# A two-layer hybrid decoder trunk on one core: negated maximum in one step, sine products on GpSimd, the last block's top-k by its dropped keys, new order tables, and pre-added residual tiles for the layer norms

## The chip, the core and the metric

The kernel runs on one core of a Trainium2 chip. The metric is the device time of one execution in microseconds (us), as a median over several runs. The profile is one execution, recorded by the hardware profiler. Engines are named as in the profile: PE is TensorE (PEld its weight loads), DVE is VectorE, ACT is ScalarE, POOL is GpSimd, SP is SyncE. A letter q behind a name (DVEq, POOLq) is that engine's instruction queue.

## The reference

There are 1024 tokens of width 1024 and two layers. A layer mixes the tokens in three groups of heads that read one input projection, maps the result by an output projection, and applies a layer norm. An MLP of width 4096 with squared ReLU and a gated input embedding follow, and a second layer norm. What the change touches is this, cut from the reference:

```
def layer_norm(x, g, b):
    mu = xf.mean(-1, keepdims=True)
    var = jnp.square(xf - mu).mean(-1, keepdims=True)
    return ((xf - mu) * lax.rsqrt(var + LN_EPS) * g + b)

def rotary(x, cos, sin):
    x1, x2 = jnp.split(x, 2, axis=-1)
    return concatenate([x1 * cos - x2 * sin, x2 * cos + x1 * sin])

def block(args):                       # 128 queries
    logits = einsum('bqhd,bsd->bqhs', iqb, ik) * IDX_DIM ** -0.5
    score = einsum('bqhs,bqh->bqs', relu(logits), iwb)
    score = where(causal, score, -inf)
    _, sel = lax.top_k(score, 256)     # 256 keys for each query
    s = einsum('bqhd,bqkd->bqhk', qb, k_sel) * HEAD_DIM ** -0.5
    pr = softmax(where(valid, s, -inf))
    return einsum('bqhk,bqkd->bqhd', pr, v_sel)

x = layer_norm(ALPHA * x + mix, ln1_g, ln1_b)
x = layer_norm(ALPHA * x + ffn + ple, ln2_g, ln2_b)
```

The other two groups of heads are a delta-rule state update over time (RWKV-7) and a pooling mixer. The change leaves their code alone, except for when their input columns are computed.

## The kernel before, in words

Activations lie transposed: features on the 128 partitions, the 1024 tokens along the free dimension in two halves of 512. Each layer is a row of stages with a meeting of all engines between them.

**The mix stage.** The input projection `z` has 17 tiles of 128 features, each done for two halves, and each half in four parts of two matmuls (`z_part`). The attention goes by blocks of 128 queries; block b sees (b+1)*128 keys. Blocks 0 and 1 see at most 256 keys and need no search. The others are searched in the order 3, 4, 5, 6, 7, 2 (`TOP_ORDER`), so block 2, with 384 keys, comes last. What is done for a block has short names:

- `iq` and `q`: PE computes the indexer's queries or the attention's queries; ACT copies them to QZ, and four DMAs on ACT's queue write them to QZS with the halves of each head swapped; DVE (`rotate`, L1589 to L1601) multiplies QZ by the cosines (L1598), QZS by the sines (L1599) and adds the two (L1601). DVE waits for the swapped copy before the first of the three.
- `lg`: for each of 8 indexer heads PE computes logits (L651), ACT takes ReLU and weight (L1212, L1220), POOL adds them up in SC (`scores`, L1379).
- `round`: DVE finds the 8 greatest of the scores (MAX8, L1611) and overwrites them with -1e30 in WK (L1613, two records: a load of the 8 values and the replacement). 32 rounds find 256 keys (`topk_round`).
- `bias`: POOL (L1469, L1471), or DVE for block 2 (L1745, L1747), turns WK and SC into 0 for a chosen key and -1e30 for another.
- `s`, for each of 6 heads: PE computes attention scores (L664). DVE (`maximum`, L1627 to L1632) adds the bias, writes the sum to PB and takes its maximum to MX, then multiplies that one column by -1/8 to NM (L1631). ACT takes the exponential with NM as bias (L1103). `pt`: PE transposes the probabilities (L671), ACT copies them (L1109). `pv`: PE multiplies by the values (L678).
- `inv`, `fin`, `sq`, `ss`, `norm`: the division by the softmax sums (L1637, L1644, L1646), the sum of squares over heads (PE L698), and the RMS norm on DVE (L1655, L1660), which reads square roots that ACT takes in two steps.
- `shift`: POOL's token shift and pooling on z tiles from the fourth on.

The order of all of it on each engine is written out in four tables (`TENSOR_ORDER`, `SCALAR_ORDER`, `VECTOR_ORDER`, `POOL_ORDER`). An engine goes through its table in that order and waits at each item for its semaphores. The buffers QZ and QZS exist once for `iq` and once for `q`; attention scores and logits share two wide PSUM buffers, one for even and one for odd heads.

**The other stages.** Preparation, the state update in 8 steps, the output projection, a layer norm, the gate, an MLP in 8 groups of 512 hidden features, and a second layer norm. The projections there split each fp32 operand into a high and a low part and use three matmuls (L1021 to L1023). DVE reads each result bank and adds it to the residual Y: L1852 behind the output projection, L1884 in the MLP; each such instruction covers one of 8 tiles for one half. POOL makes the low part of each weight block (L1502).

**The layer norm**, five times in a run (one before the first layer): PE takes the mean by 8 accumulating matmuls of the mean matrix with Y for each half (L601). DVE subtracts it (L1525). ACT squares the first half's tiles, POOL the second half's (L1353); PE adds the squares (L606), ACT takes the square root (L1072), DVE the reciprocal (L1532), and a chain of multiplications on DVE and ACT gives the result. PE does both halves' means before the first sum of squares:

```
for hf in range(2):
    for kt in range(KT):
        mm = e.matmul(BK_[4 + hf], mean_ones, Y[:, kt, hs(hf)], start=kt == 0, stop=kt == KT - 1)
    mm.then_inc(ln_mu, 1)
for hf in range(2):
    for kt in range(KT):
        e.wait_ge((ln_sq, ln_sq_later)[hf], u * KT + (kt + 1))
        e.matmul(BK_[6 + hf], mean_ones, SQ[:, 2 * hf + kt % 2, :], ...)
```

## Time and profile before

| | us |
|---|---|
| median of 3 runs | 3779.99 |
| lowest and highest | 3774.95, 3780.49 |
| the profiled execution, its own time | 3774.45 |
| its span, first to last instruction | 3772.6 |
| PE busy | 3427.3 (91% of the span) |
| DVE busy | 1784.7 (47%) |
| POOL busy | 1121.2 (30%) |
| ACT busy | 1068.7 (28%) |
| mean granted clock of TensorE | 0.954 of full |

In us from the start of the span, the mix stage of the first layer lies at 63 to 621, its state update at 660 to 872, its output projection at 903 to 1002, its two layer norms behind 1002 and behind 1866; the mix stage of the second layer lies at 1913 to 2474. The share of busy time is an average over stages that have different limits, so the rows below are mostly of one stage each. Matmul records overlap one another, and fp32 matmuls leave two records each.

### The profile page before, as it was taken

How to read it: one execution, taken by the hardware profiler on the slowest of the kernel's cores; microseconds unless marked ns; L12 is line 12 of the kernel's file. 1: busy time of each engine (PE TensorE's matmuls, PEld its weight loads, DVE VectorE, ACT ScalarE, POOL GpSimd, SP SyncE). 2: the span in 40 equal slices, each digit the busy share in tenths (PEclk: the TensorE clock that was granted, in tenths of full speed). 3: DMA queues.
4: the chain of work that ended last, by engine and by line, in shares of the span. 5: the costliest groups of instructions: out<-in, count | busy, mean ns of one | idle time of the engine just before them, and what ended most of it. 6: DMA issues, size and time to landing. Idle time of an engine off the chain costs nothing.

```text
span 3772.6 us, 61018 instructions
## 1 busy us (share of the span) xinstructions
PE 3427.3 (91%) x23080; PEld 2462.0 (65%) x23080; DVE 1784.7 (47%) x3061; ACT 1068.7 (28%) x1875; POOL 1121.2 (30%) x940
## 2 busy tenths in 40 slices
PE   7889887898999999999988888779889999999997
PEld 3444444886667888888734445458765688888884
DVE  5689996344342222222348899844335122222224
ACT  3343224443122111122133432244412112122122
POOL 1274341651212222222114543335412222222221
PEclk9999998998999999999999998889999999999998
DMA  3100000000101111111111000000011111111111
GB/s 119 38 27 22 19 20 18 1 0 20 59 12 56 50 50 44 44 53 47 34 49 39 11 22 21 18 19 0 1 34 49 35 51 44 50 45 50 50 39 45
DMA packets 43864, 132.74 MB, mean 35 GB/s; under 512 B 9280, under 2 KB 11840, under 8 KB 43072
## 3 DMA queue, kind: packets, MB, share of 16 engines
q1 hardware_dynamic: 37280, 122.41, 10.0%
q10 hardware_dynamic: 6432, 8.40, 0.9%
q8 instruction: 84, 1.38, 0.2%
q14 instruction: 68, 0.56, 0.1%
HBM read 117.15 MB, written 5.24 MB: 32 GB/s over the span
## 4 chain that ended last, share of the span: by engine, by line
PE 59%; DVE 14%; DVEq 11%; issue 10%; ACT 2%; POOLq 2%; POOL 1%; ACTq 1%; DMA 0%; SPq 0%
PE bank L1021 14%; PE bank L1023 14%; PE bank L1022 14%; DVEq L1615 8%; DVE M L1611 8%; PE bank L751 3%; PE bank L629 2%; PE wide L601 2%; DVE PB L1627 2%; PE wide L751 1%; PE wide L606 1%; DVEq L1612 1%; DVE WK L1613 1%; PE bank L719 1%; POOLq L1503 1%
## 5 line engine op out<-in xcount | busy, mean ns | idle before, releaser
L1502 POOL TENSOR_TENSOR WL<-WR,WH 128x1024 fp32r<-128x1024 f32 x160 | 389.8, 2436 | 1492.0 <-ACT WH L1305 1491.3
L629 PE MATMUL bank<-X,WR 128*128 128x512 f32 x1088 | 532.2, 633 | 19.2 <-ACT A L1189 9.9
L1021 PE MATMUL bank<-XH,WH 128*128 128x512 f32 x1280 | 517.4, 404 | 19.8 <-DVE XL L1548 10.2
L1023 PE MATMUL bank<-XH,WL 128*128 128x512 f32 x1280 | 501.5, 392 | 0.0
L1022 PE MATMUL bank<-XL,WH 128*128 128x512 f32 x1280 | 501.5, 392 | 0.0
L1884 DVE TENSOR_TENSOR Y<-Y,bank 128x512 f32<-128x512 f32 x256 | 175.9, 687 | 492.1 <-PE bank L1023 492.1
L1021 PE MATMUL bank<-HH,WH 128*128 128x512 f32 x1024 | 400.4, 391 | 0.0
L1023 PE MATMUL bank<-HH,WL 128*128 128x512 f32 x1024 | 398.6, 389 | 0.0
L1022 PE MATMUL bank<-HL,WH 128*128 128x512 f32 x1024 | 398.4, 389 | 0.0
L629 PEld LDWEIGHTS bank<-X,WR 128*128 128x128 f32 x1088 | 206.0, 200 | 270.6 <-issue 243.8
L1305 ACT ACTIVATE WH<-WR 128x1024 fp32r<-128x1024 f32 x160 | 168.2, 1053 | 736.3 <-PE bank L1023 727.7
L1871 DVE TENSOR_TENSOR RB<-RB 128x512 f32<-128x512 f32 x128 | 88.5, 692 | 561.1 <-ACT RB L1331 561.1
L1611 DVE MAX8 M<-WK 128x8 f32<-128x512 f32 (+5 forms) x372 | 331.6, 891 | 23.0 <-issue 0.9
L1613 DVE MATCH_REPLACE8 WK<-M,WK 128x512 f32<-128x512 f32 (+5 forms) x372 | 325.8, 876 | 2.3 <-issue 2.3
L1021 PEld LDWEIGHTS bank<-XH,WH 128*128 128x128 f32 x1280 | 242.2, 189 | 85.9 <-DVE XL L1548 19.7
L1022 PEld LDWEIGHTS bank<-XL,WH 128*128 128x128 f32 x1280 | 242.4, 189 | 56.5 <-issue 7.7
L1023 PEld LDWEIGHTS bank<-XH,WL 128*128 128x128 f32 x1280 | 242.2, 189 | 51.4
L1379 POOL TENSOR_TENSOR SC<-SC,R 128x512 f32<-128x512 f32 (+5 forms) x84 | 141.2, 1681 | 295.2 <-ACT R L1220 279.5
L1021 PEld LDWEIGHTS bank<-HH,WH 128*128 128x128 f32 x1024 | 192.2, 188 | 45.7 <-DVE HL L1875 6.4
L1331 ACT ACTIVATE RB<-bank 128x512 f32<-128x512 f32 x128 | 76.5, 598 | 511.2 <-PE bank L1023 511.2
L1023 PEld LDWEIGHTS bank<-HH,WL 128*128 128x128 f32 x1024 | 192.2, 188 | 40.4
L1022 PEld LDWEIGHTS bank<-HL,WH 128*128 128x128 f32 x1024 | 192.2, 188 | 39.6
(275 smaller groups left out, 5141.7 us busy)
## 6 DMA issues: line engine op xcount, KB each, us to landing
WR<-in_w SPq DMA_DIRECT2D x128, 512.0 KB, 3.5
WR<-in_w_in SPq DMA_DIRECT2D x34, 512.0 KB, 3.5
WR<-in_w_out SPq DMA_DIRECT2D x16, 512.0 KB, 3.5
WR<-in_w_gate SPq DMA_DIRECT2D x16, 512.0 KB, 5.8
Y<-in_xT SPq DMA_DIRECT2D x2, 2048.0 KB, 13.1
out_T<-X SPq DMA_DIRECT2D x1, 4096.0 KB, 11.8
QZS<-QZ ACTq DMA_DIRECT2D x48, 64.0 KB, 2.0
QZS<-QZ ACTq DMA_DIRECT2D x64, 48.0 KB, 2.0
```

The source lines that it names most:

```text
L629: mm = e.matmul(BK_[hf], WR[:, i % RING, kt, :], X[:, kt, hs(hf)], start=kt == 0, stop=kt == KT - 1)
L751: mm = e.matmul(BK_[bank][chunk(c), j * CH:(j + 1) * CH], lhs[chunk(c), 2 * j + g, :], rhs[chunk(c), 2 * j + g, :], start=True, stop=True)
L1021: e.matmul(BK_[b], WH[:, s, w, :], high[:, kt, q], start=kt == 0, stop=False)
L1022: e.matmul(BK_[b], WH[:, s, w, :], low[:, kt, q], start=False, stop=False)
L1023: mm = e.matmul(BK_[b], WL[:, s, w, :], high[:, kt, q], start=False, stop=kt == kts - 1)
L1305: e.activation(WH[:, split_seq(i) % 2, :, :], WR[:, i % RING, :, :], ACT.Copy).then_inc(w_high, 1)
L1379: e.tensor_tensor(SC[:, sl, 0:n], SC[:, sl, 0:n], R[:, w, 0:n], ALU.add).then_inc(relu_used, 1)
L1502: e.tensor_tensor(WL[:, s, :, :], WR[:, i % RING, :, :], WH[:, s, :, :].bitcast(F32), ALU.subtract)
L1611: e.max(M8[:, :], src)
L1613: e.match_replace(work, M8[:, :], src, BIG)
L1615: e.drain()
L1884: e.tensor_tensor(Y[:, i, hs(hf)], Y[:, i, hs(hf)], BK_[b], ALU.add).then_inc(d_free[b], 1)
```

## The change

Four things change in the mix stage, and one around the layer norms.

1. **Negated maximum in one step.** The instruction at L1627 scales by -1/8 and takes the minimum, so that it writes the negated maximum to NM itself. The column multiplication at L1631 goes; the drain before it stays and now signals `max_ready`.
2. **Sine products on GpSimd.** `rotate` is split: `iqc`/`qc` is the cosine product (DVE no longer waits there for the swapped copy), `iq`/`q` in DVE's table is the sum. The sine product is an item of POOL's table.
3. **Dropped keys in the 384-key block.** For block 2, the scores are copied negated and reversed to WK, and 16 rounds find the 128 keys that are dropped; one instruction turns this into the bias, reading WK reversed.
4. **New order tables** for all four engines.
5. **Residual tiles pre-added.** Behind each result read by DVE in the output projection and in the MLP, DVE also adds the Y tile to a running sum for its half (7 additions for each half; in all 8 groups of the MLP, the last of which counts). PE then takes each half's mean by one matmul of that sum, in four of the five layer norms.

```
-            def layer_norm(u, landed=None):
+            def layer_norm(u, landed=None, sums=None, total=None):
...
+                    else:
+                        e.wait_ge(ln_sum, sums + (hf + 1))
+                        mm = e.matmul(BK_[4 + hf], mean_ones, total[:, hf, :], start=True, stop=True)
...
-                for b in range(4):
-                    e.wait_ge(d_free[b], L * D_USES + (N_WOUT // 2 + 1))
-                layer_norm(L * 2 + 1)
+                layer_norm(L * 2 + 1, sums=L * LN_SUMS, total=RB)
...
-                for b in range(4):
-                    e.wait_ge(d_free[b], L * D_USES + (D_USES + 1))
-                layer_norm(L * 2 + 2)
+                layer_norm(L * 2 + 2, sums=L * LN_SUMS + 2 * FB, total=RST)
...
+            def add_to_sum(total, kt, hf):
+                if kt == 0:
+                    return
+                e.drain()
+                q = hs(hf)
+                ins = e.tensor_tensor(total[:, hf, :], Y[:, 0, q] if kt == 1 else total[:, hf, :], Y[:, kt, q], ALU.add)
+                if kt == KT - 1:
+                    ins.then_inc(ln_sum, 1)
...
POOL
+                    elif kind in ("iq", "q"):
+                        e.wait_ge(tables_landed, L * 32 + 32)
+                        e.wait_ge(swapped[kind], 64 * (rotations(L, (kind, b)) + 1))
+                        e.tensor_tensor(QZS[:, k, 0:n, :], QZS[:, k, 0:n, :], spread(ST[:, b * P:(b + 1) * P], n),
+                                        ALU.mult).then_inc(sined[kind], 1)
...
rotate, on DVE
-                e.wait_ge(swapped[kind], 64 * (rotations(L, use) + 1))
-                e.tensor_tensor(dst[:, :, :], QZ[:, k, 0:n, :], spread(CT[:, q], n), ALU.mult)
-                e.tensor_tensor(QZS[:, k, 0:n, :], QZS[:, k, 0:n, :], spread(ST[:, q], n), ALU.mult)
-                e.drain()
+                if part == "cos":
+                    e.wait_ge(turned.free, turned.read(L, use))
+                    e.tensor_tensor(dst[:, :, :], QZ[:, k, 0:n, :], spread(CT[:, q], n), ALU.mult)
+                    e.drain()
+                    return
+                e.wait_ge(sined[kind], rotations(L, use) + 1)
                 e.tensor_tensor(dst[:, :, :], dst[:, :, :], QZS[:, k, 0:n, :], ALU.add).then_inc(rotated[kind], 1)
...
topk_round
+                drop = b == TOP_ORDER[-1]
+                src = work if i or drop else SC[:, s, 0:n]
+                    if drop:
+                        e.tensor_scalar(work, SC[:, s, 0:n][:, ::-1], -1.0, None, ALU.mult)
+                        e.drain()
-                e.match_replace(work, M8[:, :], src, BIG)
-                if i < ROUNDS - 1:
+                e.match_replace(work, M8[:, :], src, DROPPED if drop else BIG)
+                if i < (ROUNDS // 2 if drop else ROUNDS) - 1:
...
maximum
-                e.tensor_tensor_reduce(out=PB[:, w, 0:n], in0=WIDE[w][:, 0:n], in1=bias, scale=1.0,
-                                       scalar=-3e38, op0=ALU.add, op1=ALU.max, accum_out=MX[:, b, h:h + 1])\
+                e.tensor_tensor_reduce(out=PB[:, w, 0:n], in0=WIDE[w][:, 0:n], in1=bias, scale=-HD ** -0.5,
+                                       scalar=3e38, op0=ALU.add, op1=ALU.min, accum_out=NM[:, b, h:h + 1])\
                  .then_inc(wide[w].free, 1)
-                e.drain()
-                e.tensor_scalar(NM[:, b, h:h + 1], MX[:, b, h:h + 1], -HD ** -0.5, None, ALU.mult)\
-                 .then_inc(max_ready, 1)
+                e.drain().then_inc(max_ready, 1)
...
bias of block 2, on DVE
-                        e.tensor_tensor(work, work, SC[:, SLOT[b], 0:n], ALU.subtract)
-                        e.drain()
-                        e.tensor_scalar(work, work, 0.0, BIG, ALU.is_equal, ALU.mult)
+                        e.tensor_scalar(SC[:, SLOT[b], 0:n], WK[:, SLOT[b], 0:n][:, ::-1], DROPPED, BIG, ALU.is_equal,
+                                        ALU.mult)
...
the end of DVE's table, before and after
-    s.7.4 s.7.5 q.2 round.2 inv.7 round.2*6 fin.7 bias.2 s.2.0 s.2.1 norm.3 norm.4 norm.5 s.2.2 s.2.3 norm.0 norm.1
-    s.2.4 norm.7 s.2.5 norm.6 inv.2 fin.2 norm.2
+    round.2*5 s.7.0 s.7.1 round.2*7 s.7.2 s.7.3 round.2*4 bias.2 s.7.4 s.7.5 qc.2 q.2 inv.7 fin.7 s.2.0 s.2.1
+    s.2.2 s.2.3 norm.5 norm.0 norm.1 s.2.4 s.2.5 norm.6 inv.2 norm.7 fin.2 norm.3 norm.4 norm.2
```

## Rows read from the trace of the kernel before

**Rows 1.** The page's chain that ended last, by engine.
```profile
PE 59%; DVE 14%; DVEq 11%; issue 10%; ACT 2%; POOLq 2%; POOL 1%; ACTq 1%; DMA 0%; SPq 0%
```

**Rows 2.** Windows: start:end, length, busy us (instructions) by engine, PE clock, DMA, GB/s.
```profile
63.00:621.00 558.00, 472.22 (x1824) 249.73 (x1824) 453.69 (x833) 189.90 (x329) 222.33 (x173) 0.92 0.09 28
...
490.00:540.00 50.00, 45.52 (x160) 22.71 (x160) 46.30 (x69) 10.30 (x20) 16.84 (x13) 1.00 0.09 25
540.00:588.00 48.00, 33.07 (x192) 23.15 (x192) 42.20 (x105) 14.24 (x20) 15.44 (x14) 0.86 0.04 12
588.00:624.00 36.00, 23.49 (x110) 12.84 (x110) 22.67 (x61) 18.46 (x39) 7.96 (x7) 0.86 0.10 26
```

**Rows 3.** PE's waits, 110 to 588 us: sum, times, longest.
```profile
PE wide L671 <- ACT PB L1103: 50.8, 22, 8.1
```

**Rows 4.** DVE, one mix stage, by form: busy us, mean ns, idle before.
```profile
L1611 DVE MAX8 M<-WK 128x8 f32<-128x384 f32 x31 | 17.3, 558 | 2.0
L1613 DVE MATCH_VALUE_LOAD WK<-M,WK 128x8 f32 x186 | 17.1, 92 | 13.6
L1613 DVE MATCH_REPLACE8 WK<-M,WK 128x384 f32<-128x384 f32 x31 | 16.8, 542 | 0.0
...
L1631 DVE TENSOR_SCALAR NM<-MX 128x1 f32<-128x1 f32 x48 | 7.4, 154 | 4.5
...
L1599 DVE TENSOR_TENSOR QZS<-QZS,ST 128x512 f32<-128x512 f32 x6 | 6.5, 1086 | 0.0
...
L1599 DVE TENSOR_TENSOR QZS<-QZS,ST 128x384 f32<-128x384 f32 x8 | 5.5, 684 | 0.0
...
L1745 DVE TENSOR_TENSOR WK<-WK,SC 128x384 f32<-128x384 f32 x1 | 0.5, 548 | 0.0
...
L1747 DVE TENSOR_SCALAR WK<-WK 128x384 f32<-128x384 f32 x1 | 0.4, 360 | 0.1
```

**Rows 5.** DVE's timeline, two maxima and the next round: start, duration.
```profile
120.20 0.15 DVE L1631 TENSOR_SCALAR NM<-MX 128x1 f32<-128x1 f32 x1
120.39 0.29 DVE L1627 CUSTOM_DVE_ANT_0 PB<-wide,C 128x128 f32<-128x128 f32 x1
120.61 0.08 DVE L1627 DVE_READ_ACCUMULATOR2_ANT MX<- 128x1 f32 x1
120.78 0.15 DVE L1631 TENSOR_SCALAR NM<-MX 128x1 f32<-128x1 f32 x1
120.85 0.68 DVE L1611 MAX8 M<-WK 128x8 f32<-128x512 f32 x1
```

**Rows 6.** The tile QZS: sums of a rotation, ns min/median/max.
```profile
L1601 DVE TENSOR_TENSOR QT<-QT,QZS x16: 557/558/1421, 91.5 to 2430.6; 128x384 f32<-128x384 f32 x16
```

**Rows 7.** DVE's timeline at the end of the mix stage.
```profile
575.07 1.22 DVE L1627 CUSTOM_DVE_ANT_0 PB<-wide,WK 128x1024 f32<-128x1024 f32 x1
...
587.70 0.42 DVE L1644 TENSOR_TENSOR A<-bank,SPR 128x256 f32<-128x256 f32 x1 [0.27 <-issue]
...
589.53 0.56 DVE L1627 CUSTOM_DVE_ANT_0 PB<-wide,WK 128x384 f32<-128x384 f32 x1 [0.30 <-issue]
```

**Rows 8.** Timelines of the layer norm at 1002 us: PE, then DVE.
```profile
1003.23 13.97 PE L601 MATMUL wide<-Y,C 128*128 128x512 f32 x32 [0.87 <-DVE Y L1852]
1017.04 9.32 PE L606 MATMUL wide<-SQ,C 128*128 128x512 f32 x20
...
1002.39 0.69 DVE L1852 SCALAR_TENSOR_TENSOR Y<-X,bank 128x512 f32<-128x512 f32 x1 [4.75 <-PE bank L1023]
...
1010.37 4.87 DVE L1525 TENSOR_TENSOR Y<-Y,wide 128x512 f32<-128x512 f32 x8 [7.29 <-PE wide L601]
...
1025.30 3.35 DVE L1532 RECIPROCAL RST<-STD 128x512 f32<-128x512 f32 x1 [3.20 <-ACT STD L1072]
```

**Rows 9.** All lines of the run: busy us, mean ns, idle before.
```profile
L1502 POOL TENSOR_TENSOR WL<-WR,WH 128x1024 fp32r<-128x1024 f32 x160 | 389.8, 2436 | 1492.0 <-ACT WH L1305 1491.3 <-issue 0.7
...
L1884 DVE TENSOR_TENSOR Y<-Y,bank 128x512 f32<-128x512 f32 x256 | 175.9, 687 | 492.1 <-PE bank L1023 492.1
```

124 lines of the change are left out of this document (64 added, 60 removed).

## The prediction

> **What bounds the kernel now.** I read the chain that ended last first: PE holds 59% of it, DVE and its queue 25% [rows 1]. So two engines set the end, each in stages of its own. The windows show where DVE does. In the mix stage, 558 us long, DVE is busy 453.7 us and PE 472.2; from 540 to 588 us DVE has 42.2 of 48 us and PE 33.1 [rows 2]. What DVE lacks there is mostly spacing between instructions: a round of the search shows 0.07 us between two of them [rows 4]. Once the rounds have begun, near 110 us, DVE is the queue that never empties. PE's own waits in that stretch confirm it: 50.8 us are waits of the transposes for the exponential [rows 3], which waits for DVE's maximum. I take the second layer's stage as equal.
>
> The reader should see a second thing in the windows: PE is not far behind. From 490 to 540 us it has 45.5 of 50 us [rows 2].
>
> In the MLP and in the output projection PE is the bound, and DVE waits for each bank: 492.1 us before 256 additions, 1.9 us each [rows 9]. In the layer norm the bound is a chain through several engines. PE takes 13.97 us for 32 records of the means, and only then comes the first sum of squares, at 1017.04; the first reciprocal starts at 1025.30 [rows 8].
>
> **The change part by part, one mix stage.**
>
> *Rounds.* One round on 384 keys is 0.558 + 0.092 + 0.542 us, with spacings of 2.0/31 and 13.6/186 us [rows 4]: 1.33 us. 16 fewer are 21.3 us off DVE's queue.
>
> *Bias and reversal of block 2.* The subtraction goes (0.548 us with 0.07 spacing), the reversed copy comes. No row has a reversed read. Its bounds are L1747's 0.36 us and L1745's 0.55 us [rows 4]; I take 0.5, and this edit is worth nothing.
>
> *Negated maximum.* L1631 costs 0.154 us and 0.09 idle, 48 times: 11.9 us is the most. But the drain stays. Start to start, L1631 holds up the next maximum by 0.19 us and the next round by only 0.07 us, since a round's first instruction starts before it ends [rows 5]. I count 24 of each kind: 6.2 us. The lower bound is 48 times 0.07, or 3.4 us.
>
> *Sine products.* Six of 512 columns at 1.086 us and eight of 384 at 0.684 us [rows 4], less 0.08 us overlap each: 10.9 us. These means hold collisions. An undisturbed product of 384 columns takes 0.56 us, as the median of the sums shows [rows 6], and then the saving is some 7.5 us (estimate, scaled by columns). The collisions will now hit the cosines and sums, so I take 10. On POOL the 14 products are about 1.3 us each, at the mean of its 173 instructions (222.3 us, rows 2): 18 us on an engine that is 40% busy there. They are hidden behind DVE's rounds if POOL comes to them in time. POOL waits for the four swap DMAs instead of DVE, and its next `lg` or `shift` items queue behind that wait; PE waits for the sum before `lg` and `s`.
>
> A sum of a rotation sometimes takes 1.42 us instead of 0.56 [rows 6], while a round keeps its time beside a busy POOL (mean 558 ns over 31, rows 4). So only some of DVE's instructions are held up by POOL. The Trainium skill (SBUF — State Buffer, the section on the shared port) says the pair of ports of DVE and GpSimd is an exclusive lock, taken when a DVE instruction has two SBUF inputs and GpSimd reads SBUF, and its Perfetto Trace Analysis page warns that moving work between the two might not help. By that rule the 14 new POOL products could block DVE's sums or cosines, but not the rounds; the rows agree on both. What it could cost is a rival below.
>
> *Together* 21.3 + 6.2 + 10 = 37.5 us less on DVE. Not all of it shortens the stage. Before, eight rounds and more lay between block 7's last maximum (575.07 to about 576.4) and its `fin` at 587.70, and hid the chain exponential, transpose, copy, `pv`, `fin`; that last one did not wait for PE [rows 7]. In the new table only a rotation and a reciprocal lie there, so this chain is open. It is at most 11.3 us; I take 7.5. DVE then needs about 8.9 us to reach block 2's first maximum, where its own work is 2.3: 6.6 us exposed. That leaves 30.9. The tail behind 589.53 lasts some 34 us. Block 2's first four maxima now come ahead of the norms, and less of `z` stands between its transposes: I put 4 us (0 to 8). PE must do its 472 us in about 526, 90% instead of 85%: I charge 3 us for maxima that come late. **32 us for each stage**, 64 for two.
>
> **The layer norms.** In front of the norm at 1002 us, DVE reads the last bank at 1002.39 [rows 8]. With the change it adds 0.69 us, a drain of 0.07 and the running sum of another 0.69: 1003.85. The first half's sum has long been done, so its mean (now one matmul in place of eight, about 0.9 us) is ready by then, and centring starts at 1003.9, not 1010.37. The greater gain is behind: the squares' matmuls no longer wait for the second mean. Before, 8.3 us passed from the first of them (1017.04) to the reciprocal (1025.30). Now the first square is there after one subtraction and one square, 1.4 us (estimate), so 1005.3 + 8.3 = 1013.6. DVE is through with its 16 subtractions at 1003.9 + 2 x 4.87 = 1013.6 too. So the reciprocal starts near 1013.8: **11.5 us earlier**. POOL's squares and everything behind shift along. Four such norms: 46 us. The norm in front of the first layer keeps its code.
>
> The additions cost nothing where they stand: 14 for each group, 0.69 us plus drain. The MLP's idle of 1.9 us before each addition [rows 9] covers them, and the output projection's 4.75 us [rows 8] more so. If POOL's weight split of 2.44 us [rows 9] stood in their way, a bank would come free some 2 us later; PE has three other banks meanwhile. Without this cover each would cost 0.76 us. The last one is in the sum above.
>
> **Sum.** 64 + 46 = 110 us. Against the profiled execution's 3774.45 that gives 3664.5. The median stands 5.5 us (0.15%) above that execution; I put **3668 us** for the median, 3% less.
>
> **Rivals.**
>
> *PE becomes the bound of the mix stage (0.20).* For: PE's best stretch is 91% [rows 2], and the new stage asks for 90% on average, with an order in which each transpose waits for an exponential. Against: PE's largest waits are for DVE [rows 3] and should shrink. If PE keeps only 87%, a stage lasts 472/0.87 = 543 us and gives 15 us: 30 + 46 = 76, or about 3700.
>
> *All of DVE's saving arrives (0.10).* The open chain is covered by the new order, and the tail gives 8 us: 45 us a stage, 136 in all, about 3640.
>
> *The layer norm's PE runs at the lower clock (0.10).* The stretch 540 to 588 us, where PE is busy 33 of 48 us, has a granted clock of 0.86 against 1.00 in the fuller one before it [rows 2]. The 13.97 us of dense means go, so the sums of squares could run at 1.2 GHz. They take 0.43 us a record now (9.32 over 20 has 0.4 idle, rows 8); at half the clock the first half's 16 take 13.8 us instead of 6.9. Each norm then gives 4.6 us, 18 in all, with 64: about 3694. The Trainium skill (TensorE: Matmul & The Clock Gate, Part 1) says that the gate halves the clock when the array has recently been idle; by it this rival is possible, and no row shows it for this place.
>
> *The shared ports (0.04).* Each of 28 rotations loses a POOL product's 1.3 us: 36 us back, about 3704.
>
> *Slower: POOL's queue (0.03).* The sine product stands behind `lg`, `bias` and `shift` items in one queue. If DVE has to wait for six POOL instructions of 1.3 us at each of 28 rotations, that is 28 x 7.8 = 218 us against 110: about 3885. It decides from 3.9 us per rotation on. Against: POOL is idle 60% of the stage [rows 2], and a rotation can be asked for early.
>
> *My forecast* has 0.53.
>
> **How the numbers follow.** The unknown terms of the forecast (maximum 3.4 to 11.9, sines 7.5 to 10.9, chain, tail 0 to 8, PE) make it 3648 to 3686. With the rivals at 3640 and 3700 inside, the range is 3634 to 3708. A measurement of this kernel can tell some 0.2% (7.6 us) from no change. Faster by more than that: all cases but the last, less a little for what I have overlooked, 0.96; within it 0.015; slower 0.025.
>
> **What would show it.** In the changed profile: 186 searches reduced to 170 in each stage; no L1631 records; DVE's busy time in a mix stage near 417 us, its length near 526; a wait of DVE of some 6 us before block 7's `fin`; the means as 4 records of PE and a first reciprocal 11.4 us behind the last bank, in place of 22.9; PE's wait for the exponential below 50.8 us. It is wrong if DVE shows waits for POOL's sine products, if PE has over 92% of the stage, or if the first reciprocal of a norm comes later than 14 us behind the last bank.

## The result, and the profile after

The changed kernel takes **3711.36 us** (median of 4 runs, 3705.19 to 3717.18), beside 3779.55 (3774.95 to 3780.49) for the kernel before in the same comparison: ratio 0.9823, 95% interval 0.9811 to 0.9835. That is 68 us faster. The forecast was 3668 in a range of 3634 to 3708, so the sign was right, the size was not, and the median lies outside the range. The profiled execution has a span of 3710.5 us at a mean granted clock of 0.951. One slow execution, of n_middve (5609 us at a mean granted clock of 0.553), is left out of that kernel's median below.

The layer norms' part of the forecast, 46 of 110 us, came in almost to the tenth. The timelines of VectorE and of TensorE at a changed layer norm (start, duration, engine, line, operation), which answer to [rows 8]:

```profile
996.02 0.69 DVE L1872 SCALAR_TENSOR_TENSOR Y<-X,bank 128x512 f32<-128x512 f32 x1 [3.97 <-PE bank L1028]
996.80 0.69 DVE L1566 TENSOR_TENSOR RB<-RB,Y 128x512 f32<-128x512 f32 x1
997.41 9.65 DVE L1532 TENSOR_TENSOR Y<-Y,wide 128x512 f32<-128x512 f32 x16
1007.18 3.35 DVE L1539 RECIPROCAL RST<-STD 128x512 f32<-128x512 f32 x1
...
995.82 1.02 PE L606 MATMUL wide<-RB,C 128*128 128x512 f32 x2
997.55 1.12 PE L606 MATMUL wide<-RB,C 128*128 128x512 f32 x2 [0.71 <-DVE RB L1566]
998.81 9.42 PE L611 MATMUL wide<-SQ,C 128*128 128x512 f32 x20
```

The means are 4 records instead of 32. The first reciprocal starts 1007.18 - 996.02 = 11.2 us behind the last bank, where it started 1025.30 - 1002.39 = 22.9 behind it: 11.75 us gained, 11.5 forecast. The other three changed norms are alike (11.2 or 11.3 us behind the last bank, 22.9 or 23.0 before), and the granted clock during the sums of squares is 1.00 in both kernels.

The mix stage is the other half. Its last row before the next stage is the setting of RSM (L1779), at 614.47 us here and at 621.12 before; in the second layer 2437.17 and 2474.13. The 37.0 us of the second row are 6.65 of the first stage, two layer norms with 23.5, and 6.8 that are left for the second stage. Measured from the first matmul of `z` to that last row, the two stages fell by 7.0 us (568.2 to 561.2) and 8.3 us (571.8 to 563.5). The forecast had 32 for each. (The profiled executions stand 62.1 us apart, 3772.6 and 3710.5 us of span, the medians 68.) The windows, as in [rows 2] (start:end, length, busy us and instructions of PE, PEld, DVE, ACT, POOL, clock, DMA share, GB/s):

```profile
63.00:614.50 551.50, 476.27 (x1824) 252.15 (x1824) 427.38 (x724) 190.63 (x330) 238.25 (x187) 0.91 0.09 28
490.00:540.00 50.00, 46.42 (x196) 25.73 (x195) 46.19 (x62) 16.66 (x32) 15.38 (x15) 0.97 0.05 15
540.00:588.00 48.00, 39.92 (x218) 25.84 (x217) 32.71 (x72) 17.43 (x29) 13.96 (x9) 0.93 0.04 12
```

The reader should compare two numbers with [rows 2]. VectorE's busy time fell by 26.3 us (453.69 to 427.38), but the stage only by 6.7. From 540 to 588 us VectorE, 42.2 of 48 us busy before, has 32.71, and TensorE has 39.92 instead of 33.07. VectorE is no longer the queue that never empties. The waits from 110 to 588 us say on whom it waits now (sum, times, longest); first VectorE's and TensorE's of the changed kernel:

```profile
DVE PB L1650 <- PE wide L669: 30.0, 12, 12.0
DVE A L1665 <- PE bank L683: 4.9, 1, 4.9
...
PE wide L676 <- ACT PB L1104: 24.2, 12, 4.3
PE wide L669 <- ACT R L1213: 12.3, 13, 1.9
```

and VectorE's wait for scores in the kernel before, from 110 us and then from 60 us on:

```profile
DVE PB L1627 <- PE wide L664: 4.4, 2, 2.9
```

```profile
DVE PB L1627 <- PE wide L664: 18.4, 3, 14.0
```

VectorE's maxima wait 30.0 us for TensorE's scores. The 4.4 us before are not the number to set against that: 12.0 of the 30.0 are the wait in front of the very first maximum, which ends at 110.1 us, and the kernel before has the same wait with 14.0 us, ending at 107.3 and so outside the window. From 60 us on the two sums are 30.0 and 18.4. TensorE's wait for the exponential fell from 50.8 [rows 3] to 24.2, and another stands beside it: 12.3 us in which a score tile of the attention (L669) finds no free wide bank, because ScalarE's rectifier (L1213) has yet to read an indexer tile out of it.

VectorE's groups of one stage, by form (busy us, mean ns, idle before), as in [rows 4]:

```profile
L1634 DVE MAX8 M<-WK 128x8 f32<-128x384 f32 x16 | 9.0, 562 | 1.3
L1636 DVE MATCH_REPLACE8 WK<-M,WK 128x384 f32<-128x384 f32 x16 | 8.7, 543 | 0.0
L1616 DVE TENSOR_TENSOR QT<-QZ,CT 128x384 f32<-128x384 f32 x8 | 7.7, 964 | 1.2 <-issue 1.2
L1616 DVE TENSOR_TENSOR IQ<-QZ,CT 128x512 f32<-128x512 f32 x6 | 6.2, 1029 | 19.3 <-ACT QZ L1200 16.4 <-ACT R L1213 2.3 <-issue 0.4
L1620 DVE TENSOR_TENSOR IQ<-IQ,QZS 128x512 f32<-128x512 f32 x6 | 5.3, 880 | 5.4 <-POOL QZS L1480 4.7
L1632 DVE TENSOR_SCALAR WK<-SC 128x384 f32<-128x384 f32 x1 | 2.4, 2444 | 0.2 <-issue 0.2
L1766 DVE TENSOR_SCALAR SC<-WK 128x384 f32<-128x384 f32 x1 | 0.4, 360 | 0.1
```

The rounds are gone as forecast, with their time for one unchanged (562 and 543 ns). The sines are off the engine, but the cosine of 384 columns takes 964 ns on average and that of 512 columns 1029, against 558 and 691 where nothing is in the way (the shortest of the sums, which have the same shapes, in the view of the tile QZS). And the reversed copy of block 2's scores, taken at 0.5 us, lasts 2444 ns.

### The profile page after: what moved, and what is told of

The parts are those of the page before. It is cut to its first block, busy times and chain, and to the rows that moved or that the text cites. A ratio compares the mean times of both kernels' runs of the same rounds, so it can differ in the third digit from the quotient of the medians.

```text
span 3710.5 us, 61088 instructions
## 1 busy us (share of the span) xinstructions
PE 3385.9 (91%) x22968; PEld 2442.8 (66%) x22968; DVE 1912.9 (52%) x3093; ACT 1069.7 (29%) x1875; POOL 1165.8 (31%) x968
## 4 chain that ended last, share of the span: by engine, by line
PE 64%; DVE 11%; issue 10%; DVEq 8%; ACT 2%; POOLq 2%; POOL 1%; ACTq 1%; DMA 1%; SPq 0%
PE bank L1026 14%; PE bank L1027 14%; PE bank L1028 14%; DVE M L1634 6%; DVEq L1638 6%; PE bank L634 4%; PE bank L756 3%; PE wide L756 2%; PE wide L611 1%; PE wide L656 1%; DVE PB L1650 1%; PE bank L724 1%; PE bank L683 1%; POOLq L1510 1%; PE bank L920 1%
## 5 line engine op out<-in xcount | busy, mean ns | idle before, releaser
L1509 POOL TENSOR_TENSOR WL<-WR,WH 128x1024 fp32r<-128x1024 f32 x160 | 402.9, 2518 | 1479.9 <-ACT WH L1306 1479.2
L634 PE MATMUL bank<-X,WR 128*128 128x512 f32 x1088 | 542.6, 647 | 19.9 <-ACT A L1190 10.6
L1905 DVE TENSOR_TENSOR Y<-Y,bank 128x512 f32<-128x512 f32 x256 | 176.0, 688 | 324.6 <-PE bank L1028 324.6
L1634 DVE MAX8 M<-WK 128x8 f32<-128x512 f32 (+5 forms) x342 | 315.3, 922 | 26.3 <-issue 1.7
L1636 DVE MATCH_REPLACE8 WK<-M,WK 128x512 f32<-128x512 f32 (+5 forms) x342 | 309.6, 905 | 1.8 <-issue 1.8
```

The source lines that it names most:

```text
L634: mm = e.matmul(BK_[hf], WR[:, i % RING, kt, :], X[:, kt, hs(hf)], start=kt == 0, stop=kt == KT - 1)
L1509: e.tensor_tensor(WL[:, s, :, :], WR[:, i % RING, :, :], WH[:, s, :, :].bitcast(F32), ALU.subtract)
L1634: e.max(M8[:, :], src)
L1636: e.match_replace(work, M8[:, :], src, DROPPED if drop else BIG)
L1905: e.tensor_tensor(Y[:, i, hs(hf)], Y[:, i, hs(hf)], BK_[b], ALU.add).then_inc(d_free[b], 1)
```

## The experiments

15 kernels, in four groups, each beside runs of the kernel before. Gains over the kernel before are the difference of the medians of one group. The changed kernel was timed in a comparison of its own, so where a run is set against it, or against a run of another group, the medians are taken as they are; the kernel before itself has medians from 3776.97 to 3781.22 us over the groups, so such a difference is uncertain by some 4 us beside its own scatter.

### Each part alone

**a_sums**: the kernel before with the pre-added residual tiles and nothing else.

```diff
+                        add_to_sum(RB, mt, hf)
-                        for kt in range(KT):
-                            mm = e.matmul(BK_[4 + hf], mean_ones, Y[:, kt, hs(hf)], ...)
+                        mm = e.matmul(BK_[4 + hf], mean_ones, total[:, hf, :], start=True, stop=True)
```

> The kernel before with the pre-added residual sums for the layer norms alone. Theory (the norms gave what was forecast, and the mix stage is what fell short): the reciprocal starts about 11.2 us behind the last bank in place of 22.9, in four norms, so 47 us less than before, near 3732, with both mix stages as long as before (558 and 561 us). Rival (part of the 47 us is paid back as added DVE work in the MLP or by a lower TensorE clock): 30 us less or smaller, and the changed kernel's mix stages then gave more than their 7 us each.

3733.72 against 3779.39 us, ratio 0.9877 (0.9862 to 0.9892): **45.7 us**, forecast 46. The rival that the norm's TensorE work drops to the lower clock is out: the 20 records of L611 above take 9.42 us, as they took 9.32, at a granted clock of 1.00 both times. The four reciprocals of this run start 11.2 or 11.3 us behind the last bank.

**c_drop**: block 2's search for the dropped keys alone, 16 rounds instead of 32, the order tables otherwise as before.

```diff
-    round.7*12 round.2*6 s.7.0 s.7.1 round.2*9 s.7.2 s.7.3 round.2*10 s.7.4 s.7.5 q.2 round.2 inv.7 round.2*6 fin.7
+    round.7*12 round.2*3 s.7.0 s.7.1 round.2*4 s.7.2 s.7.3 round.2*5 s.7.4 s.7.5 q.2 round.2 inv.7 round.2*3 fin.7
```

> The kernel before with block 2 searched by its dropped keys alone, in the old order tables with 16 items less (3, 4, 5, 1 and 3 rounds around block 7's maxima in place of 6, 9, 10, 1 and 6). Theory A (DVE's queue bounds the stage up to the end, as forecast): 21 us less in each stage minus an exposed chain of some 6 us, so about 30 us for the run. Theory B (near the end of the stage the chain of block 7's softmax over PE, ACT and DVE sets the pace as soon as rounds go): 10 us a stage or less, and DVE shows new waits for PE's scores of block 7 in about the sum of what is missing.

3749.79 us, ratio 0.9922 (0.9908 to 0.9935): **29.6 us**. The forecast's working gives 2 x (21.3 - 6.6) = 29.4. The number agrees, but the 6.6 us go elsewhere here. The old table still has four rounds between block 7's last maximum and its `fin`, so the chain in front of `fin` stays covered: VectorE waits 0.5 us there. What is new are waits of maxima for TensorE's scores from 539 us on, of which the kernel before has none:

```profile
DVE PB L1632 <- PE wide L665: 7.6, 3, 4.3
```

From block 3's first round to its end the first stage is 13.9 us shorter (511.1 to 497.2), which is 21.3 less 7.4. So the saving ends in waits for TensorE, the sign of my Theory B, in about the amount that the forecast had put on another wait. That the sum fits to 0.2 us is luck.

**b_negmax**: the negated maximum in one step, L1631 gone.

```diff
-                                       scalar=-3e38, op0=ALU.add, op1=ALU.max, accum_out=MX[:, b, h:h + 1])
-                e.tensor_scalar(NM[:, b, h:h + 1], MX[:, b, h:h + 1], -HD ** -0.5, None, ALU.mult)
+                                       scalar=3e38, op0=ALU.add, op1=ALU.min, accum_out=NM[:, b, h:h + 1])
```

> The kernel before with the negated maximum in one step alone; the 96 column multiplications go. Theory (the drain and the semaphore that stay set the spacing: in the changed trace the next maximum still starts 0.37 us behind the accumulator's read, as before): no difference that can be measured, under 2 us for the whole run. Rival (the forecast's term): 6.2 us for each mix stage, 12 us in all. A second rival: ACT gets the maximum 0.2 us earlier and PE's transposes follow, which would show as some us less wait of PE for the exponential.

3771.47 us, ratio 0.9984 (0.9975 to 0.9993): **8 us** (3 to 9 by the interval), forecast 12.4, and my expectation here, under 2 us, was too low. The changed kernel's timeline shows that VectorE got nearly nothing of it:

```profile
122.39 0.29 DVE L1650 CUSTOM_DVE_ANT_0 PB<-wide,C 128x128 f32<-128x128 f32 x1 [0.35 <-PE wide L669]
122.61 0.08 DVE L1650 DVE_READ_ACCUMULATOR2_ANT NM<- 128x1 f32 x1
122.98 0.29 DVE L1650 CUSTOM_DVE_ANT_0 PB<-wide,C 128x128 f32<-128x128 f32 x1 [0.29 <-issue]
123.20 0.09 DVE L1650 DVE_READ_ACCUMULATOR2_ANT NM<- 128x1 f32 x1
123.42 0.69 DVE L1634 MAX8 M<-WK 128x8 f32<-128x512 f32 x1
```

From the accumulator's read to the next maximum 122.98 - 122.61 = 0.37 us pass. In the kernel before the same spacing is 0.37 us too, with L1631 in it, as the median of the 17 such pairs that its stage's timeline holds. To the next round it is 123.42 - 123.20 = 0.22 against 120.85 - 120.61 = 0.24 us [rows 5]. So the small instruction stood in a gap that is there anyway. What is left is that its signal to ScalarE goes off some 0.2 us earlier, 48 times a stage. The trace of b_negmax has the sign that the expectation's second rival named: TensorE waits for the exponential 48.1 and 48.6 us in the two stages (windows 110:588 and 1963:2441), the kernel before 50.8 and 52.8, and a_sums, whose mix stage is that of the kernel before, 51.8 and 51.2. The stages are 2.5 and 1.7 us shorter from block 3's first round to their end. So the gain goes by way of ScalarE, as far as can be told; no run holds that signal back, and the rest of the 8 us is not placed.

**d_sine**: the sine products on GpSimd alone.

```diff
-                e.tensor_tensor(QZS[:, k, 0:n, :], QZS[:, k, 0:n, :], spread(ST[:, q], n), ALU.mult)
+                e.wait_ge(sined[kind], rotations(L, use) + 1)
```

> The kernel before with the sine products on POOL alone; DVE's table has cosine and sum next to each other where the rotation was, POOL's table has each sine product behind the item that precedes it on ACT. Theory (the products' time comes back as collisions: in the changed trace cosines of 384 columns take 964 ns in place of 558 and those of 512 take 1029 in place of 804): DVE gains 4 to 5 us a stage and loses about as much in waits for POOL, so within 10 us of before for the run. Rival (the forecast's term): 10 us a stage, 20 in all. Rival on the other side: POOL's waits for the swap copies hold up its scores, and the run is over 10 us slower.

3766.59 us, ratio 0.9969 (0.9957 to 0.9981): **12.8 us**, forecast 20. Two rows of its first stage say what became of the difference (by form, window 60:621):

```profile
L1610 DVE TENSOR_TENSOR IQ<-IQ,QZS 128x512 f32<-128x512 f32 x6 | 7.4, 1242 | 7.7 <-POOL QZS L1480 7.1
L1606 DVE TENSOR_TENSOR QT<-QZ,CT 128x384 f32<-128x384 f32 x8 | 4.6, 580 | 0.2 <-issue 0.2
```

Here the cosines keep their times (580 and 789 ns, before 558 and 804), and it is the sums of 512 columns that take 1242 ns instead of 708. All of the rotations' instructions together take 21.4 us of VectorE instead of 30.8, so 9.4 us less where the products alone were 12.0. Of the wait for GpSimd's products 2.4 us lie behind block 3's first round. From that round to its end the stage is 6.5 and 5.5 us shorter in the two layers.

### The order tables

**t_tables**: the four new tables on the kernel before, with block 2's rounds doubled back to 32 and the sines where they were.

```diff
-    z.0.0*4 z.1.0*4 iq.3 z.2.0*4 q.0 z.3.0*4 q.1 vt.0 lg.3.0 lg.3.1 z.0.1 lg.3.2 lg.3.3 z.0.1 ...
+    z.0.0*4 z.1.0*4 iq.3 z.2.0 q.0 z.2.0*3 q.1 z.3.0*4 lg.3.0 lg.3.1 vt.0 z.0.1*2 lg.3.2 lg.3.3 z.0.1 ...
```

> The kernel before with the new order tables alone (rotations whole again, 32 rounds for block 2, spread 10, 14 and 8 around block 7's maxima). The four edits alone gave 46, 6, 30 and 13 us, 95 together, and the whole change gave 68. Theory (the new tables cost what is missing): 20 to 30 us slower than before, near 3805, with DVE waiting for PE's scores in the middle of the stage. Rival (the edits overlap, the tables are neutral): within 8 us of before.

3805.56 against 3778.68 us, ratio 1.0074 (1.0054 to 1.0094): **27 us slower**. For the tables the forecast had a gain of 1 us a stage.

**f_oldorder**: all edits, with the old tables adapted (block 2's rounds as in c_drop, `iqc` and `qc` put directly in front of `iq` and `q`, the sines in GpSimd's table at the old places of the rotations).

```diff
-    iq.3 q.0 z.2.0 vt.0 ...
+    iqc.3 iq.3 z.2.0 qc.0 q.0 vt.0 ...
```

> All edits of the change with the old order tables, adapted: 16 rounds less for block 2, cosine and sum where the rotation was, the sine products put into POOL's table. Theory (the new tables are at fault): the four gains add up, 95 us less than before, near 3685 and 25 us below the changed kernel. Rival (the gains overlap, since the mix stage has a floor near 545 us that PE and the softmax chain set): as the changed kernel, near 3711.

3694.68 us, ratio 0.9781 (0.9769 to 0.9794): 84 us faster than before, and **17 us faster than the changed kernel**; the two intervals against before don't touch. The expectation had 95 us if the gains add up and 68 if they overlap; it is between the two.

**g_nosine** is the same with the sines left on VectorE, **e_sine_dve** the changed kernel with them put back.

> As the run with all edits in the old tables, but with the sine products on DVE as before. If the gains add up, this is slower than that run by the 13 us that the products gave alone, near 3698. If the products' gain needs DVE to be the bound, and it no longer is with 16 rounds less, the two are equal.

> The changed kernel with the sine products back on DVE, in the new tables. Theory (with the new tables DVE waits for PE for some 30 us a stage, so its own work matters less): within 6 us of the changed kernel's 3711. Rival (DVE's work still counts in full): 13 us more, near 3724.

3700.56 us (0.9795, 0.9782 to 0.9808) and 3720.38 us (0.9846, 0.9833 to 0.9858). Beside the other edits the sines' move is worth 6 us with the old tables and 9 with the new ones, in both cases between the two values that the expectations had named.

**i_vt**: one suspect of the new tables, the place of `vt.0`.

```diff
-    z.3.0*4 lg.3.0 lg.3.1 vt.0 z.0.1*2
+    z.3.0*4 vt.0 lg.3.0 lg.3.1 z.0.1*2
```

> The changed kernel with one item moved: the value projection vt.0 goes ahead of lg.3.0 and lg.3.1 in TensorE's table, where it stands in the kernel before. If the later start of the new tables comes from that item (the first copy of V on VectorE at 97.3 us instead of 92.5, the GpSimd weights of lg.3.1 and the first round of block 3 behind it, 60.9 us from the first z matmul instead of 57.1), the first round comes 3 to 4 us earlier in each mix stage and the kernel takes 3704 (3702 to 3707). Rival: lg.3.0 or the exponentials of ScalarE set the start, and the middle of the stage waits for TensorE anyway: 3711 as the changed kernel.

3715.83 us, ratio 0.9819 (0.98 to 0.9837), as the changed kernel. The expected 7 us did not come. The first round comes 61.8 us behind the first matmul of `z` in the first stage and 63.0 in the second, where the changed kernel has 60.9 and 63.9. But the start of the first stage has two lengths in one and the same code, by the clock that the execution got there. This run's window, the changed kernel's, and that of m_mid (below), which has the changed kernel's start (columns as above):

```profile
60.00:70.00 10.00, 6.90 (x14) 2.82 (x13) 1.22 (x3) 7.10 (x10) 0.00 (x0) 0.83 0.36 123
```

```profile
60.00:70.00 10.00, 6.58 (x17) 2.65 (x16) 0.21 (x1) 5.62 (x8) 0.00 (x0) 1.00 0.48 176
```

```profile
60.00:70.00 10.00, 6.61 (x11) 2.61 (x10) 0.00 (x0) 5.39 (x7) 0.00 (x0) 0.72 0.51 186
```

The right comparison is with executions that got less than the full clock there too:

| start of the tables | runs | first stage, full clock | first stage, part of it lower | second stage |
|---|---|---|---|---|
| old | before; f_oldorder, h_split | 57.1 | 60.2, 60.2 | 60.9; 61.9, 61.6 |
| new | changed; m_mid, t_tables | 60.9 | 63.7, 63.7 | 63.9; 65.2, 64.7 |
| new, `vt.0` earlier | i_vt | | 61.8 | 63.0 |

(us from the first matmul of `z` to block 3's first round). So the new start does cost, 3 to 4 us a stage, and moving `vt.0` gives back 1 to 2 of them, half of what I had expected. Two stages make some 3 to 4 us for the run, which this run's interval, some 7 us to either side, can't tell from none.

**h_split**: the old tables up to the end of block 5's attention, the new ones behind it.

> All edits; the order tables are the old ones (adapted) up to the end of block 5's attention, and the new ones from there on. It tells which half of the new tables costs the 17 us by which the changed kernel is slower than the one with the old tables (3694.7). Theory (first half: later start and TensorE's scores late in blocks 1 to 4): 3694 to 3699. Rival (second half: blocks 6, 7 and 2, with the softmax chain open before block 7 ends): 3707 to 3711.

3686.66 against 3781.22 us, ratio 0.9751 (0.9735 to 0.9767): the lowest median of all, 94.6 us below the kernel before, and lower than my theory had it. The new tail costs nothing, the price is in the first part. Whether the new tail also gains is open: the median is 8 us below f_oldorder's and j_flip's, but its five runs go from 3685.03 to 3693.81, its interval overlaps with j_flip's, and its profiled execution (span 3692.0 us) is level with f_oldorder's (3692.4). In these two traces block 2's first round lies 68.5 and 70.8 us ahead of the stage's end with the new tail, 71.1 and 71.2 with the old.

**m_mid**: the changed kernel with the old middle, from block 1's second tile to the end of block 4's attention. The core of it on TensorE:

```diff
-    z.6.1*4 z.7.0*3 s.4.0 s.4.1 z.7.0 lg.6.2 lg.6.3 z.7.1 pt.4.0 z.7.1*2 pt.4.1 pv.4.0 pv.4.1 lg.6.4 lg.6.5 s.4.2 s.4.3
-    z.7.1 lg.6.6 lg.6.7 z.8.0 pt.4.2 z.8.0 pt.4.3 iq.2 pv.4.2 pv.4.3 s.4.4 s.4.5 z.8.0 pt.4.4
+    q.5 z.7.0 lg.6.2 lg.6.3 z.7.0 s.4.0 s.4.1 ss.3 z.7.0 pt.4.0 pt.4.1 pv.4.0 pv.4.1 lg.6.4 lg.6.5 z.7.0 s.4.2 s.4.3
+    z.7.1 pt.4.2 pt.4.3 lg.6.6 pv.4.2 z.7.1 pv.4.3 lg.6.7 s.4.4 z.7.1 s.4.5 pt.4.4
```

> The changed kernel, with the old tables' items in the middle of each mix stage alone (all four engines, from block 1's second tile to the end of block 4's attention); start, blocks 5 and 6 and the tail stay new. Theory (the middle holds what the new tables cost: block 4's to block 7's first rounds came 9.7 us later in the stage than with the old tables): 3695 (3690 to 3700). Rival (the cost is spread, or lies in blocks 5 and 6 behind the cut): 3703 to 3711.

3699.16 against 3776.97 us, ratio 0.9788 (0.9774 to 0.9801): **12 us faster than the changed kernel** (10 us, if each is set against its own runs of the kernel before), from the middle alone. Where in the stage it comes from is read from the first round of each block. The timelines, the first rounds of block 4 and of block 7; of the changed kernel:

```profile
190.94 0.79 DVE L1634 MAX8 M<-SC 128x8 f32<-128x640 f32 x1
...
444.78 1.23 DVE L1634 MAX8 M<-SC 128x8 f32<-128x1024 f32 x1 [0.23 <-issue]
```

and of m_mid:

```profile
194.49 0.78 DVE L1634 MAX8 M<-SC 128x8 f32<-128x640 f32 x1
...
438.05 1.23 DVE L1634 MAX8 M<-SC 128x8 f32<-128x1024 f32 x1 [0.23 <-issue]
```

253.8 us against 243.6. The same stretch, taken in the same way, is 245.8 in the kernel before, 256.0 in t_tables, 244.2 in f_oldorder and 242.1 in h_split; in the second layer 253.8 (changed), 245.2 (m_mid), 244.5, 250.3, 240.4 and 242.1. So the new middle makes it 6 to 13 us longer, whatever edits stand beside it. A part of that is only work moved into the stretch: from block 3's first round to block 4's the changed kernel needs 76.8 us, m_mid 77.9 and f_oldorder 79.1. From block 3's first round to block 7's both kernels have the same number of TensorE's records, and the middle costs 9 us a stage (9.3 here, 8.7 in the second). The windows of that longer stretch, the changed kernel and m_mid:

```profile
114.12:444.78 330.66, 293.54 (x1083) 152.01 (x1083) 280.36 (x481) 116.84 (x199) 162.43 (x124) 0.89 0.09 27
```

```profile
116.64:438.05 321.41, 289.20 (x1083) 150.81 (x1082) 279.50 (x481) 116.67 (x199) 162.46 (x124) 0.92 0.10 28
```

Of the 9.3 us TensorE spends 4.3 in longer work, at a granted clock of 0.89 instead of 0.92, and 4.9 idle (37.1 us against 32.2); in the second stage it is 5.5 and 3.2. The two together are 18 us for the run where the medians differ by 12: in the profiled executions m_mid gives 2.5 us back at the start of the first stage, where it had the lower clock, and 3.6 behind the second mix stage. What fills the idle time: between 190 and 447 us the changed kernel's VectorE waits for scores, and TensorE for the rectifier (the views of the waits; first the changed kernel):

```profile
DVE PB L1650 <- PE wide L669: 7.9, 4, 4.0
...
PE wide L669 <- ACT R L1213: 8.3, 8, 1.9
```

and m_mid:

```profile
DVE PB L1650 <- PE wide L669: 1.9, 2, 1.4
...
PE wide L669 <- ACT R L1213: 3.1, 3, 1.4
```

6.0 us of VectorE's waits for scores and 5.2 of TensorE's for a wide bank go. The lower mean clock says that a larger part of TensorE's work in the changed kernel ran at 1.2 instead of 2.4 GHz; that those waits brought the clock down is likely, but no run shows it.

**n_middve** and **o_midpe** split the middle by engine: the old items in VectorE's table alone, and in the other three alone.

> As the run before, but VectorE's table alone has the old middle; TensorE, ScalarE and GpSimd keep the new one. Theory (TensorE's new order sets it: two score tiles of the attention in a row among the indexer's logits, so that a logit tile waits for ScalarE's rectifier to free one of two wide banks, and the clock falls in those waits): no gain, 3707 to 3716. Rival (VectorE asks for its maxima at a bad place): 3695 to 3700.

> The counterpart: TensorE, ScalarE and GpSimd have the old middle, VectorE keeps the new one. Theory (TensorE's order sets it): 3695 to 3700, as with all four. Rival (VectorE's places set it): 3707 to 3716.

3752.17 us (0.9932, 0.9919 to 0.9945) and 3767.44 us (0.9974, 0.9964 to 0.9984). Both expectations failed, and the kernels are 41 and 56 us slower than the changed one. From 190 to 460 us their maxima wait for scores; n_middve, then o_midpe:

```profile
DVE PB L1650 <- PE wide L669: 28.1, 9, 10.0
```

```profile
DVE PB L1650 <- PE wide L669: 28.6, 4, 11.6
DVE IQ L1616 <- ACT R L1213: 10.4, 2, 8.8
```

So neither engine's order is the bad one by itself. The tables are a matched set: as I read these waits, a maximum must be asked for when its score tile is done and not before. Half a set costs three to five times what m_mid gained by changing both halves.

### The reversed copy

**j_flip**: f_oldorder with the reversed copy moved one round earlier, ahead of block 7's last round, whose end starts GpSimd's bias.

```diff
-fin.6 round.7*12 round.2*3 s.7.0
+fin.6 round.7*11 flip.2 round.7 round.2*3 s.7.0
```

> The kernel with all edits and the old tables, with the reversed negated copy of block 2's scores made one round of block 7 earlier, so that GpSimd's bias of block 7 isn't started by the same signal. Theory: the 2.44 us of that copy are a stand-off of the two engines at their common port, and alone it takes about 0.4: 2 us of VectorE per stage are free, and the run takes 3691 to 3693 against 3694.7, if TensorE's scores of block 7 don't simply end the gain in a wait (then 3694.7). Rival: a reversed read that also writes a bfloat16-free copy is slow by itself, the copy stays at 2.4 us wherever it stands, and the time stays 3694.7.

First f_oldorder's timelines of VectorE and GpSimd at that place:

```profile
533.00 2.44 DVE L1632 TENSOR_SCALAR WK<-SC 128x384 f32<-128x384 f32 x1 [0.23 <-issue]
...
539.82 1.22 DVE L1650 CUSTOM_DVE_ANT_0 PB<-wide,WK 128x1024 f32<-128x1024 f32 x1 [0.39 <-issue]
...
532.88 2.34 POOL L1470 TENSOR_TENSOR WK<-WK,SC 128x1024 f32<-128x1024 f32 x1 [15.03 <-DVEq L1640]
535.38 3.66 POOL L1472 TENSOR_SCALAR WK<-WK 128x1024 f32<-128x1024 f32 x1 [0.16 <-issue]
```

then j_flip's:

```profile
529.83 0.36 DVE L1764 TENSOR_SCALAR WK<-SC 128x384 f32<-128x384 f32 x1 [0.19 <-issue]
...
539.41 1.23 DVE L1647 CUSTOM_DVE_ANT_0 PB<-wide,WK 128x1024 f32<-128x1024 f32 x1 [2.42 <-POOL WK L1472]
...
532.96 2.36 POOL L1470 TENSOR_TENSOR WK<-WK,SC 128x1024 f32<-128x1024 f32 x1 [15.57 <-DVEq L1637]
535.48 3.66 POOL L1472 TENSOR_SCALAR WK<-WK 128x1024 f32<-128x1024 f32 x1 [0.16 <-issue]
```

Alone the copy takes 0.36 us. Beside GpSimd's subtraction, which had started 0.12 us before it, it takes 2.44 and ends when that one has ended (532.88 + 2.34 = 535.22 against 535.44), while the subtraction keeps its 2.34 to 2.36 us. One engine stood still for the other; they didn't share. The Trainium skill (SBUF — State Buffer, "Who interferes with whom") lists `tensor_scalar` among the operations that can take both of VectorE's ports and so be locked out for the whole of a GpSimd instruction; the two timelines agree with it.

The time stayed: 3694.85 us, ratio 0.977 (0.9753 to 0.9787), beside 3694.68 without the move. The second timeline says why. Block 7's first maximum needs the bias, which GpSimd ends at 539.14. The 2 us that VectorE no longer loses in the copy it now waits in front of that maximum (2.42 us), three rounds later. The expectation had named such an end of the gain, but as a wait for TensorE's scores; it is one for GpSimd's bias.

**k_best**: j_flip, with `s.2.2` ahead of the norms of blocks 3 and 4, and `s.2.3` ahead of block 5's.

```diff
-bias.2 s.2.0 s.2.1 norm.3 norm.4 norm.5 s.2.2 s.2.3 norm.0 norm.1 s.2.4
+bias.2 s.2.0 s.2.1 s.2.2 norm.3 norm.4 s.2.3 norm.5 norm.0 norm.1 s.2.4
```

> The same as the run with the earlier reversed copy, and in the tail of VectorE's table s.2.2 goes ahead of the norms of blocks 3 and 4, and s.2.3 ahead of norm.5, so that the wait of 3.7 us for ScalarE's square root holds up no maximum. If the tail hangs on that wait: 3687 to 3691. Rival: ScalarE's exponentials of block 2 bound the tail, and it is as the run with the earlier copy alone.

3702.47 us, ratio 0.9787 (0.9769 to 0.9805), 8 us slower than j_flip. VectorE's timeline:

```profile
571.95 0.56 DVE L1647 CUSTOM_DVE_ANT_0 PB<-wide,SC 128x384 f32<-128x384 f32 x1 [1.91 <-PE wide L669]
...
580.53 0.56 DVE L1647 CUSTOM_DVE_ANT_0 PB<-wide,SC 128x384 f32<-128x384 f32 x1 [8.02 <-PE wide L669]
...
581.52 0.95 DVE L1673 RECIPROCAL RSD<-RSD 128x128 f32<-128x128 f32 x1 [0.42 <-issue]
```

The wait of 3.7 us for the square root had been the cheaper one. In its place the maximum waits 8.02 us for TensorE's tile, with three norms queued behind it. From block 2's first round to the stage's end k_best needs 79.0 us, j_flip 73.2.

## Why the prediction was right and wrong

| term | forecast | alone | beside the others |
|---|---|---|---|
| layer norms | 46 | 45.7 (a_sums) | 11.75 each by the trace |
| rounds less the opened chain | 29.4 | 29.6 (c_drop) | |
| negated maximum | 12.4 | 7.9 (b_negmax) | |
| sines | 20 | 12.8 (d_sine) | 6 to 9 (g_nosine, e_sine_dve) |
| tables: other order in the tail, late maxima | 8 - 6 = 2 | -27 (t_tables) | -17 (f_oldorder) |
| sum | 110 | 69 | 68 measured |

**Layer norms: right.** The working by timelines, the cover for the additions, and the drop of the second mean from the squares' path all hold. The additions cost nothing: VectorE's idle ahead of the MLP's additions went from 492.1 [rows 9] to 324.6 us, and the run still gained the full 46.

**Rounds: right in size, in part by luck.** The saving of 1.33 us a round holds. In the changed kernel the wait in front of block 7's `fin` is there at 4.9 us, where the forecast had some 6.6 exposed. But c_drop, whose 29.6 us stand in the table, has that chain covered and loses 7.6 us to waits for TensorE's scores, which the forecast's term did not hold.

**The order tables: the step that failed.** The forecast took the tables' effect to be two corrections, "I put 4 us (0 to 8)" for the tail and "I charge 3 us for maxima that come late", and never went through the middle of the tables, though they were rewritten from the first line to the last. Alone they cost 27 us, and beside the other edits 17 against f_oldorder and 25 against h_split. The runs place this: 9 us a stage in the middle, from block 3's first round to block 7's (changed kernel against m_mid), and 3 to 4 us a stage in the start, which the forecast did not look at either (the table under i_vt); for two stages that is 24 to 26 us, the distance to h_split. It is not that TensorE was full, the reason that the forecast gave for its 3 us: it is busy 476.27 of 551.5 us, 86%. In the middle half of the price is TensorE's idle time, with maxima and wide banks waiting for each other, and half is work at the lower clock. The tail's term of 4 us stays open: the trace of the changed kernel shows none of it (from block 2's first round to the stage's end 71.1 us with the new tail, 71.1 with the adapted old one), the median of h_split would allow it. The sum of VectorE's waits for scores is a poor guide here. From 114 to 588 us it is 4.4 us before, 16.8 in the changed kernel, but also 15.9 in m_mid and 13.4 in f_oldorder, since a VectorE with less to do comes to its maxima earlier.

**Negated maximum: mechanism wrong, and the bounds held by luck.** "L1631 holds up the next maximum by 0.19 us" read the start to start distance as the instruction's price. Without it the next maximum starts no earlier (0.37 us in both kernels), and the next round by 0.03 us. 7.9 us came nevertheless, below the forecast's 12.4 and in its bounds of 6.8 to 23.8, and what the traces show of them is ScalarE's earlier start, which the forecast did not count.

**Sines: size.** 12.8 us for 20. The collisions that had lengthened the sines went over to their neighbours: in d_sine to the sums of 512 columns (6 x 0.53 = 3.2 us a stage), in the changed kernel, with other places in the tables, to the cosines (964 and 1029 ns where 558 and 691 are undisturbed: 8 x 0.41 + 6 x 0.34 = 5.3 us). The forecast had named this and taken off 0.9 us for it; the 2.4 us of waits for GpSimd it had at nothing. The rounds kept their times, so by the rows the collisions hit products and sums of two tiles in SBUF and the reversed copy, and leave the search alone. The Trainium skill (SBUF — State Buffer, "Who interferes with whom") has it so for instructions with two inputs in SBUF. Beside the other edits still less is left, since VectorE is no longer the bound everywhere (argued from the waits).

**The reversed copy: size, but free.** 2.44 us where 0.5 was taken, outside its bounds of 0.36 and 0.55. It cost no time in the old tables (j_flip), since VectorE had to wait for the bias anyway; with the new ones this was not tried.

**Overlap.** The four edits alone give 96 us, together with the old tables 84, and with the old tables up to block 5 and the new tail 95 (h_split). So the overlap is 12 us in one order and 1 in another, and since each of the five medians is uncertain by 3 to 6 us, the 12 are not far from the noise. I read them as the forecast's rival of TensorE in a smaller size; that is argued, not shown. It put 543 us to a stage in which TensorE keeps 87%; f_oldorder's window reads

```profile
63.00:606.60 543.60, 473.57 (x1824) 248.84 (x1824) 423.23 (x723) 190.22 (x330) 238.01 (x187) 0.93 0.09 29
```

that is 87%, in 543.6 us. But it isn't bound by TensorE alone: both engines idle, each for the other. As a book-keeping of medians, the account of the forecast's 110 - 68 = 42 us is then: the tables 17 + 2, the overlap 12, the maximum 4.5, the sines 7.2, together 43.

**Of the tests named:** the searches fell by 16 (176 rounds for 192; the rows' count of 186 leaves out the first round of each block), no L1631, means and reciprocal as said, the wait for the exponential below 50.8, all right. VectorE's busy time of 427 instead of 417, and a stage of 551 instead of 526, were the first signs of what had failed. Waits for GpSimd's sines do appear, which the forecast had named as a sign of being wrong: 6.5 us for two of them at the stage's start. At that size the rival of GpSimd's queue is out, since it needed 3.9 us for each of 28 rotations.

**Small slips of the working**, none of which moves the verdict: 110 us off a median of 3780 make 3670, not 3668; seven rounds and a rotation, not eight rounds, stood between block 7's last maximum and its `fin`; and of the 24 pairs of each kind that it counted behind L1631 the stage's trace holds 17 and 18.

## What to carry to other kernels

When a change rewrites a static order for several engines, cost the order by itself, first of all by running it alone on the old code: here it took back 17 of 84 us, and the best kernel of the study (3686.66 us) keeps all of the edits and the first part of the old order. A saving on the engine that never idles is worth its full size only until the next engine's waits begin: of 21.3 us of rounds a stage, 7.6 ended in waits for TensorE. Sums of waits can only be compared over the same items, not over the same clock times. And before a difference of some us is read from one trace, look at the granted clock of the same stretch in both. A small instruction in a chain is priced by taking it out of the spacing between its neighbours, not by its duration.

## What the runs showed that I had not expected

A reversed read costs VectorE nothing: 128 x 384 f32 with a step of -1 takes 0.36 us (L1764 of j_flip, L1766 of the changed kernel), as the forward one did [rows 4], as long as GpSimd leaves it alone, and 2.44 us otherwise. After an accumulator's read the next maximum starts 0.37 us later, whether or not a 128 x 1 instruction stands between them. The start of the first mix stage has two lengths some 3 us apart in the same code (old tables 57.1 or 60.2 us, new ones 60.9 or 63.7), with the granted clock at 1.00 or at 0.72 to 0.83 in its window from 60 to 70 us. And half of a matched set of order tables cost 41 to 56 us against the changed kernel, about twice what the whole change had brought in the two mix stages (68 less the norms' 46).
